# Linear attention: key decays of all eight sub-blocks by one subtraction and one exponential per direction, no clears by GpSimd

## The chip, the cores and the metric

One Trainium2 chip, one core of it. The metric is the device time of the whole program in microseconds (us), the median of several executions. The core's engines work side by side and wait for one another through semaphores: TensorE (PE, matrix products; its weight loads are PEld), VectorE (DVE), ScalarE (ACT), GpSimd (POOL) and SyncE (SP, which only issues transfers here).

## The reference, cut to what matters

The program is two model blocks, one after the other, over 512 tokens of width 1024. The first has two layers (`l` = 0, 1). Each layer mixes tokens in four branches (a short convolution, gated linear attention, latent attention, a wide convolution), and then runs a feed-forward network. The second block has a state-space mixer and a mixture of 32 experts. The change concerns only the gated linear attention of the two layers, which runs in both directions over the sequence:

```python
b = jnp.cumsum(ac, axis=2)                      # running sum of log decays, per key channel
rel = b[:, :, :, None, :] - b[:, :, None, :, :]
decay = jnp.where(mask5, jnp.exp(jnp.where(mask5, rel, 0.0)), 0.0)
scores = jnp.einsum('bhtk,bhsk,bhtsk->bhts', qc, kc, decay)
```

Four heads of 32 key channels lie on the 128 partitions. A score of query t and key s is a sum over channels of q·k·exp(b[t] − b[s]). To make it a matrix product, the exponential is split at an anchor a: exp(b[t] − b[a]) goes to the query, exp(b[a] − b[s]) to the key.

## The kernel before, in words

Tokens lie along the free dimension in four blocks of 128 (`j` = 0 to 3, `TB` = 4), and inside a block in eight sub-blocks of 16 (`SUB`, `NSUB`), each with an anchor of its own. `cpos` holds the running sums of both directions `d`, and `kdec[:, d, i, s]` the key decays of direction d against the anchor of sub-block i, for the 128 keys of the block: 128 partitions x 1024 elements per direction.

The order of work is written out by hand: each engine has one instruction stream, in program order, and nothing overtakes. For each `j` the streams are:

- **ScalarE** (lines 1317 to 1360): for both directions eight exponentials into `kdec`, one for each sub-block (L1327), each with the anchor as its bias and only over the keys that the sub-block may see (16, 32, ... 128 columns). For j = 0 they wait for GpSimd's clear of that half of `kdec`, later for the products that read it (`gdiag` of j − 1). Then the exponentials `khat` and `qhat` for the pairs of different blocks (L1337, L1340), then at j = 0 and 1 copies of values (L1282), then the copies of the off-diagonal scores from PSUM (L1352, L1357), which wait for TensorE. At j = 2 the copy of a projection `gg0` (L1235) comes behind them; at j = 3 three square roots (L1202) come ahead of them.
- **VectorE** (lines 1960 to 2009): `kdec` is bounded and multiplied by the keys in one instruction per direction (L1965, `scalar_tensor_tensor` with `min` and `mult`), then `khat` and `qhat` are multiplied (L1973, L1976). Then comes side work: `centre` at j = 0, squares at j = 1 and 2 (L1990), modulation values at j = 2 (L1726). Then the diagonal scores are masked out of PSUM (L1998) and the two directions added (L2003). L2009 marks that all scores are there.
- **TensorE** (lines 741 to 782): values of the tokens (`token_values`), a mean, then for each j eight products `gdiag` per direction (a 128 x 128 slice of `kdec` against 64 columns of `qdiag`), the off-diagonal `goff`, and side work behind them: `token_values` at j = 0, `modulation` (weights against 2 columns) at j = 1, the projection `gg0` at j = 2, `gg1` at j = 3. At j = 3 three variances stand between `gdiag` and `goff`. All of these have line 589 in the profile, where the helper `mm` records them. A float32 product stands in the trace as two records.
- **GpSimd** (lines 456 to 462): clears `qdiag`, and then the two halves of `kdec`, once per layer (L460 and L462). The never-written parts of `kdec` stay zero from then on. The region of `kdec` is shared with the buffers `score` and `probs` of the softmax attention that runs before, so the second clear waits for the last transposition (`turn`, L734), which reads `probs`.

`BOUND` is 1e30. The mask of L1998 sets every score of a forbidden pair to zero.

Of the kernel before, what the change touches and what calls it, by code (L numbers as in the profile page):

```python
# [9 lines left out]
P = 128  # L10
T = 512
TB = T // P
# [5 lines left out]
HEADS = 4  # L18
# [5 lines left out]
SUB = 16  # L24
# [111 lines left out]
def build(nc, io, marks, found):  # L136
    with ExitStack() as ctx:
# [311 lines left out]
        def _(pool):  # L449
# [6 lines left out]
            for l in range(DEPTH):  # L456
                pool.wait_ge(dve_done, when("query", l, HEADS - 1))
                nc.gpsimd.memset(qdiag, 0.0).then_inc(pool_done, did.up(("qdiag_zero", l)))
                pool.wait_ge(act_done, when("exps", l, HEADS * TB - 1))
                nc.gpsimd.memset(kdec[:, 0], 0.0).then_inc(pool_done, did.up(("kdec_zero", l, 0)))  # L460
                pool.wait_ge(pe_done, when("full", "turn", l, HEADS * TB - 1))
                nc.gpsimd.memset(kdec[:, 1], 0.0).then_inc(pool_done, did.up(("kdec_zero", l, 1)))  # L462
            pool.wait_ge(pe_done, when("full", "up", DEPTH - 1, KF - 1, 1))
            pool.dma_start(hc, io["ctx"].rearrange("p (k t) -> p k t", t=CTX)).then_inc(s_ctx, 16)
            pool.wait_ge(act_done, when("norm_out", ("ln2", DEPTH - 1), KD - 1))
# [722 lines left out]
        def _(act):  # L1188
# [42 lines left out]
            for l in range(DEPTH):  # L1231
# [84 lines left out]

                for j in range(TB):
                    for d in range(2):
                        if j == 0:
                            act.wait_ge(pool_done, when("kdec_zero", l, d))  # L1320
                        else:
                            act.wait_ge(pe_done, when("full", "gdiag", l, j - 1, d))
                        for i in range(NSUB):
                            a = j * P + i * SUB + (0, SUB - 1)[d]
                            s0, s1 = ((0, (i + 1) * SUB), (i * SUB, P))[d]
                            act.wait_ge(act_done, did.n)
                            nc.scalar.activation(kdec[:, d, i, s0:s1], cpos[:, d, j * P + s0:j * P + s1], ACT.Exp,  # L1327
                                bias=cpos[:, d, a:a + 1], scale=-1.0).then_inc(act_done, did.up(*([("kdec_exp", l, j,
                                d)] if i == NSUB - 1 else [])))
                    for d in range(2):  # L1330
                        if 0 < (TB - 1 - j, j)[d]:
                            a = (j * P + P - 1, j * P)[d]
                            t0, t1 = (((j + 1) * P, T), (0, j * P))[d]
                            if j >= 2:
                                act.wait_ge(pe_done, when("full", "goff", l, j - 2, HEADS - 1))
                            act.wait_ge(act_done, did.n)
                            nc.scalar.activation(khat[:, d, j % 2, :], cpos[:, d, j * P:(j + 1) * P], ACT.Exp,  # L1337
                                bias=cpos[:, d, a:a + 1], scale=-1.0).then_inc(act_done, did.up())
                            act.wait_ge(act_done, did.n)
                            nc.scalar.activation(qhat[:, d, j % 2, t0:t1], cpos[:, d, t0:t1], ACT.Exp, bias=cneg[:,  # L1340
                                d, a:a + 1]).then_inc(act_done, did.up(("qhat_exp", l, j, d)))
                    if j < 2:
                        keep_values(2 * j)
                    if j == TB - 1:
                        for i, tag in enumerate((("cfm", l), ("branch", l, 0), ("branch", l, 2))):
                            deviation(tag, out=deviations[:, i, :])
                    for h in range(HEADS):
                        act.wait_ge(pe_done, when("full", "goff", l, j, h))
                        src = bank_of("goff", l, j, h)
                        if j > 0:  # L1350
                            act.wait_ge(act_done, did.n)
                            nc.scalar.activation(amat(h)[:, j, 0:j * P], src[:, 0:j * P],  # L1352
                                ACT.Copy).then_inc(act_done, did.up(*([("free", "goff", l, j,
                                h)] if j == TB - 1 else [])))
                        if j < TB - 1:
                            act.wait_ge(act_done, did.n)
                            nc.scalar.activation(amat(h)[:, j, (j + 1) * P:T], src[:, (j + 1) * P:T],  # L1357
                                ACT.Copy).then_inc(act_done, did.up(("free", "goff", l, j, h)))
                    if j == TB - 2:
                        keep("gg0")  # L1360
# [356 lines left out]
        def _(dve):  # L1717
# [109 lines left out]
            for l in range(DEPTH):  # L1827
# [127 lines left out]
                for c in range(2):  # L1955
                    dve.wait_ge(dve_done, did.n)
                    nc.vector.tensor_tensor(y[:, c, :], y[:, c, :], proj[:, SLOT["b0"] + c, :],
                        ALU.mult).then_inc(dve_done, did.up(("ya", l)))

                for j in range(TB):  # L1960
                    kj = proj[:, SLOT["k"], j * P:(j + 1) * P]
                    for d in range(2):
# [20 lines left out]
                    if j in (1, 2):  # L1983
                        dve.wait_ge(act_done, when("yc", l, HEADS - 1))
                        for tag, src, dst in (((("cfm", l), proj[:, 0:2, :], early_squares["cfm"]),
                                               (("branch", l, 0), y[:, 0:2, :], early_squares[0])) if j == 1 else
                                              ((("branch", l, 2), y[:, 4:6, :], early_squares[2]),)):
                            for k in range(2):
                                dve.wait_ge(dve_done, did.all_but(1))
                                nc.vector.tensor_tensor(dst[:, k, :], src[:, k, :], src[:, k, :], ALU.mult).then_inc(  # L1990
                                    dve_done, did.up(("square", tag, k)))
                        dve.wait_ge(dve_done, did.n)
                    for d, mask in enumerate((const("upto"), const("after"))):
                        dve.wait_ge(pe_done, when("full", "gdiag", l, j, d))
                        src = bank_of("gdiag", l, j, d)[:].rearrange("p (i h t) -> p h i t", h=HEADS, t=SUB)
# [728 lines left out]
```

## Time and profile before

| | us |
|---|---|
| median of 3 runs | 3659.97 (3656.41 to 3660.52) |
| the profiled execution, its own time | 3656.11 |
| its span in the trace | 3654.3 |
| PE busy | 3439.4 (94%) |
| DVE busy | 2409.4 (66%) |
| ACT busy | 1713.0 (47%) |
| POOL busy | 492.3 (13%) |

All times of rows are counted from the start of the span. The linear attention of layer 0 lies at about 245 to 330 us, that of layer 1 at about 1065 to 1150 us. In a timeline a row is: start, duration, engine, line, operation, output and inputs, shapes, count; in brackets how long the engine was idle before it, and what ended that. Granted clock 1.00 is 2.4 GHz of TensorE, 0.50 is 1.2 GHz.

### The profile page before, as it was taken

The page shows a single profiled execution, that of the slowest core. Times are in us where ns is not written, and L with a number is a line of the kernel's source. Part 1 is how long each engine was busy: PE and PEld are TensorE (multiplying, and loading weights), DVE is VectorE, ACT ScalarE, POOL GpSimd, SP SyncE. Part 2 cuts the span into 40 slices and gives each one's busy share as a digit, 9 for nine tenths or more (in the row PEclk, how much of TensorE's full clock was granted, in tenths as well). Part 3 has the DMA queues.
Part 4 walks back from the last instruction along what each step waited for, and adds up shares of the span by engine and source line. Part 5 has one row for each costly group of instructions (what it writes and reads, how often), then busy time and mean ns, then how long its engine had stood idle before and what let it go on. Part 6 is the DMA issues. An engine that isn't in the chain of part 4 may idle for free.

```text
span 3654.3 us, 43770 instructions
## 1 busy us (share of the span) xinstructions
PE 3439.4 (94%) x13658; PEld 2393.2 (65%) x13658; DVE 2409.4 (66%) x2948; ACT 1713.0 (47%) x2318; POOL 492.3 (13%) x630
## 2 busy tenths in 40 slices
PE   7989999999988999998998889989999999999996
PEld 3445588874344588875654554378887888888884
DVE  3565464553564464555556874179999999999995
ACT  2344232232344332233321113168888888888884
POOL 0000000000000000000000000024343433334340
PEclk9988999999988999999998999999999999999998
DMA  4100233332110233332111002169999999999995
GB/s 180 52 31 28 81 116 115 113 101 69 52 35 23 87 112 113 116 114 71 52 52 58 24 24 92 63 245 372 355 375 347 369 367 365 369 355 376 352 372 182
DMA packets 167697, 618.86 MB, mean 169 GB/s; under 512 B 18496, under 2 KB 18624, under 8 KB 166880
## 3 DMA queue, kind: packets, MB, share of 16 engines
q1 hardware_dynamic: 156768, 573.84, 43.7%
q0 software_dynamic: 10816, 43.52, 4.2%
q8 instruction: 70, 1.15, 0.1%
q14 instruction: 43, 0.35, 0.0%
HBM read 587.92 MB, written 29.36 MB: 169 GB/s over the span
## 4 chain that ended last, share of the span: by engine, by line
PE 53%; issue 21%; POOL 11%; DVE 9%; ACT 3%; POOLq 2%; DMA 1%; DVEq 0%; SPq 0%; ACTq 0%
PE bank L589 51%; POOL pick L555 2%; POOL sb_work L501 2%; POOL y_rows L561 1%; DVE sb_rstd L1737 1%; DVE sb_work L1779 1%; POOL sb_work L507 1%; POOL picks_e L508 1%; POOL sb_work L547 1%; POOLq L514 1%; POOL sb_work L549 1%; POOLq L513 1%; ACT sb_work L1327 1%; POOL sb_work L544 1%; DVE sb_work L2259 0%
## 5 line engine op out<-in xcount | busy, mean ns | idle before, releaser
L2462 DVE TENSOR_TENSOR w_part<-sb_ring,w_part 128x1024 fp32r<-128x1024 f32 x762 | 890.1, 1225 | 63.1 <-ACT w_part L1641 38.9
L1641 ACT ACTIVATE w_part<-sb_ring 128x1024 fp32r<-128x1024 f32 x762 | 770.5, 1054 | 80.5 <-PE bank L1126 47.7
L1126 PE MATMUL bank<-w_part,xg_hi 128*128 128x512 f32 x2048 | 564.1, 397 | 0.0
L589 PE MATMUL bank<-h_hi,split_part 128*128 128x512 f32 x1408 | 447.5, 403 | 4.8 <-ACT h_hi L1409 4.8
L1126 PEld LDWEIGHTS bank<-w_part,xg_hi 128*128 128x128 f32 x2048 | 383.1, 188 | 89.1
L589 PE MATMUL bank<-sb_work,sb_ring 128*128 128x512 f32 (+5 forms) x880 | 331.4, 531 | 4.0 <-ACT sb_rstd L1202 2.5
L1126 PE MATMUL bank<-w_part,xg_lo 128*128 128x512 f32 x1024 | 321.2, 395 | 0.0
L589 PEld LDWEIGHTS bank<-h_hi,split_part 128*128 128x128 f32 x1408 | 267.2, 191 | 69.2 <-ACT h_hi L1409 5.1
L1126 PE MATMUL bank<-w_part,act_hi 128*128 128x512 f32 x1024 | 284.9, 400 | 2.0 <-DVE act_lo L2505 0.9
L589 PE MATMUL bank<-sb_hT,sb_ring 128*128 128x512 f32 (+1 forms) x608 | 272.5, 606 | 9.6 <-ACT sb_hT L1218 9.6
L589 PE MATMUL bank<-h_lo,split_part 128*128 128x512 f32 x704 | 272.1, 393 | 0.0
L589 PEld LDWEIGHTS bank<-sb_work,sb_ring 128*128 128x128 f32 (+4 forms) x880 | 162.8, 187 | 163.1 <-issue 150.6
L589 PE MATMUL bank<-sb_work 128*128 128x64 f32 (+6 forms) x992 | 228.8, 414 | 30.9 <-DVE sb_work L1965 13.7
L589 PE MATMUL bank<-act_hi_ff,split_part 128*128 128x512 f32 x704 | 229.9, 408 | 5.7 <-DVE act_lo_ff L2089 5.7
L1402 ACT ACTIVATE split_part<-sb_ring 128x1024 fp32r<-128x1024 f32 x136 | 142.7, 1052 | 194.2 <-PE bank L589 194.2
L1126 PEld LDWEIGHTS bank<-w_part,xg_lo 128*128 128x128 f32 x1024 | 192.6, 188 | 46.5
L589 PEld LDWEIGHTS bank<-sb_hT,sb_ring 128*128 128x128 f32 (+1 forms) x608 | 116.6, 193 | 160.2 <-issue 157.9
L1126 PEld LDWEIGHTS bank<-w_part,act_hi 128*128 128x128 f32 x1024 | 187.4, 188 | 45.4 <-issue 4.3
L1449 ACT ACTIVATE sb_work<-bank 128x512 f32<-128x512 f32 x88 | 52.7, 599 | 339.4 <-PE bank L589 335.9
L589 PEld LDWEIGHTS bank<-sb_work 128*128 128x128 f32 (+3 forms) x992 | 141.6, 218 | 100.1 <-issue 44.8
L589 PE MATMUL bank<-sb_xT,sb_ring 128*128 128x512 f32 (+2 forms) x416 | 187.9, 607 | 11.8 <-ACT sb_xT L1218 11.8
L2047 DVE TENSOR_TENSOR split_part<-sb_ring,split_part 128x1024 fp32r<-128x1024 f32 x136 | 165.9, 1221 | 20.2 <-ACT split_part L1402 20.0
(350 smaller groups left out, 4630.2 us busy)
## 6 DMA issues: line engine op xcount, KB each, us to landing
sb_ring<-in_w SPq DMA_DIRECT2D x768, 512.0 KB, 7.4
sb_ring<-in_wstream SPq DMA_DIRECT2D x304, 512.0 KB, 3.5
y_rows<-sb_padc POOLq DMA_DIRECT2D x1, 4096.0 KB, 27.4
sb_xT<-in_x SPq DMA_DIRECT2D x1, 2048.0 KB, 11.6
x_rows<-sb_padc SPq DMA_DIRECT2D x1, 2048.0 KB, 22.7
residual<-sb_hT POOLq DMA_DIRECT2D x1, 2048.0 KB, 6.6
sb_hT<-residual POOLq DMA_DIRECT2D x1, 2048.0 KB, 8.2
x_rows<-sb_work SPq DMA_DIRECT2D x1, 2048.0 KB, 7.0
```

Of the source, the lines that this page charges most:

```text
L501: nc.gpsimd.tensor_tensor(passed[:, n:n + 1], slot_row[:, 0:1], slot_row[:, 0:1], ALU.add).then_inc(moe_pool_done, turn_did.up())
L507: nc.gpsimd.tensor_copy(rank_e.unsqueeze(2), rank[:, :, bass.ds(e, 1)]).then_inc(mark, turn_did.up())
L508: nc.gpsimd.tensor_copy(picks_e[:], picks[:, :, bass.ds(e, 1), :].bitcast(F32).rearrange("p b e c -> p b (e c)")).then_inc(mark, turn_did. ...
L513: e = pool.value_load(table[0:1, 0, bass.ds(i + ahead, 1)], min_val=0, max_val=EXPERTS - 1)
L555: nc.gpsimd.tensor_scalar(pick[:, b, :], slots, rank_e[:, b:b + 1], None, ALU.is_equal).then_inc(moe_pool_done, turn_did.up(("pick",)))
L589: ins = nc.tensor.matmul(out, l, r, start=start, stop=stop)
L1126: ins = nc.tensor.matmul(out[n][:], l[:, k, :], r[:, n * 512:(n + 1) * 512], start=False, stop=(k, p) == (KD - 1, 2))
L1402: nc.scalar.activation(split_hi[t % NSPLIT], ring[:, n % RING, :], ACT.Copy).then_inc(act_done, did.up(("w_hi", l, t)))
L1449: nc.scalar.activation(ubuf[:, i % 4, 1:T + 1], bank_of("up", l, c, v)[:], ACT.Copy).then_inc(act_done, did.up(("free", "up", l, c, v), (" ...
L1641: nc.scalar.activation(w_hi[t % SPLITS], ring[:, t % RING, :], ACT.Copy).then_inc(s_hi, 1)
L2047: nc.vector.tensor_tensor(split_lo[t % NSPLIT], ring[:, n % RING, :], split_hi[t % NSPLIT].bitcast(F32), ALU.subtract).then_inc(dve_done, ...
L2462: nc.vector.tensor_tensor(w_lo[t % SPLITS], ring[:, t % RING, :], w_hi[t % SPLITS].bitcast(F32), ALU.subtract).then_inc(s_lo, 1)
```

## The change

GpSimd no longer clears `kdec`. A new function `key_args(j)` on VectorE subtracts, in one instruction per direction, the anchors of all eight sub-blocks from the block's 128 running sums, into all 1024 elements of `kdec[:, d]`. ScalarE then takes one exponential per direction over these 1024 elements, in place, with no bias. `key_args(0)` stands ahead of the loop over j on VectorE; `key_args(j + 1)` stands in turn j behind the side work and ahead of the masks of L1998. It waits for the products that read `kdec` (`gdiag` of the turn before it), or for j = 0 for the last transposition. The positions that used to stay zero now get an exponential as well, which L1965 bounds and the mask removes.

```diff
@@ gpsimd
-                pool.wait_ge(act_done, when("exps", l, HEADS * TB - 1))
-                nc.gpsimd.memset(kdec[:, 0], 0.0).then_inc(pool_done, did.up(("kdec_zero", l, 0)))
-                pool.wait_ge(pe_done, when("full", "turn", l, HEADS * TB - 1))
-                nc.gpsimd.memset(kdec[:, 1], 0.0).then_inc(pool_done, did.up(("kdec_zero", l, 1)))
@@ scalar
                 for j in range(TB):
                     for d in range(2):
-                        if j == 0:
-                            act.wait_ge(pool_done, when("kdec_zero", l, d))
-                        else:
-                            act.wait_ge(pe_done, when("full", "gdiag", l, j - 1, d))
-                        for i in range(NSUB):
-                            a = j * P + i * SUB + (0, SUB - 1)[d]
-                            s0, s1 = ((0, (i + 1) * SUB), (i * SUB, P))[d]
-                            act.wait_ge(act_done, did.n)
-                            nc.scalar.activation(kdec[:, d, i, s0:s1], cpos[:, d, j * P + s0:j * P + s1], ACT.Exp,
-                                bias=cpos[:, d, a:a + 1], scale=-1.0).then_inc(act_done, did.up(*([("kdec_exp", l, j,
-                                d)] if i == NSUB - 1 else [])))
+                        act.wait_ge(dve_done, when("kdec_arg", l, j, d))
+                        nc.scalar.activation(kdec[:, d], kdec[:, d], ACT.Exp, scale=-1.0).then_inc(act_done,
+                            did.up(("kdec_exp", l, j, d)))
@@ vector
+                def key_args(j):
+
+                    for d in range(2):
+                        pos = cpos[:, d, j * P:(j + 1) * P]
+                        anchor = pos.rearrange("p (i s) -> p i s", s=SUB)[:, :, (0, SUB - 1)[d]:(1, SUB)[d]]
+                        if j == 0:
+                            dve.wait_ge(pe_done, when("full", "turn", l, HEADS * TB - 1))
+                        else:
+                            dve.wait_ge(pe_done, when("full", "gdiag", l, j - 1, d))
+                        dve.wait_ge(dve_done, did.n)
+                        nc.vector.tensor_tensor(kdec[:, d], pos.unsqueeze(1).to_broadcast([P, NSUB, P]),
+                            anchor.to_broadcast([P, NSUB, P]), ALU.subtract).then_inc(dve_done,
+                            did.up(("kdec_arg", l, j, d)))
+
+                key_args(0)
                 for j in range(TB):
...
+                    if j + 1 < TB:
+                        key_args(j + 1)
                     for d, mask in enumerate((const("upto"), const("after"))):
                         dve.wait_ge(pe_done, when("full", "gdiag", l, j, d))
```

## Rows read from the trace of the kernel before

**Rows 1.** Page of the profile: the chain that ended last, by engine.

```profile
PE 53%; issue 21%; POOL 11%; DVE 9%; ACT 3%; POOLq 2%; DMA 1%; DVEq 0%; SPq 0%; ACTq 0%
```

**Rows 2.** L1965 in both layers: its waits, then its waiters (us, times).

```profile
  ACT sb_work L1327: 74.3, 16
...
  PE bank L589: 13.7, 6
```

**Rows 3.** Timeline of PE, layer 0.

```profile
244.79 5.53 PE L589 MATMUL bank<-sb_work 128*64 128x512 f32 x8 [0.69 <-ACT sb_work L1267]
...
273.43 3.13 PE L589 MATMUL bank<-sb_work 128*128 128x64 f32 x32 [1.07 <-DVE sb_work L1965]
...
284.10 8.70 PE L589 MATMUL bank<-sb_work 128*128 128x64 f32 x48 [0.63 <-DVE sb_work L1965]
292.73 8.95 PE L589 MATMUL bank<-sb_hT,sb_ring 128*128 128x512 f32 x16
...
328.52 4.13 PE L589 MATMUL bank<-sb_sq,sb_work 128*64 128x512 f32 x13
```

**Rows 4.** Timeline of ACT, layer 0.

```profile
250.37 0.59 ACT L1274 ACTIVATE sb_xT<-bank 64x512 f32<-64x512 f32 x1 [5.62 <-PE bank L589]
251.05 6.24 ACT L1327 ACTIVATE sb_work<-sb_work 128x16 f32<-128x16 f32 x16
...
265.87 6.24 ACT L1327 ACTIVATE sb_work<-sb_work 128x16 f32<-128x16 f32 x16
...
279.66 6.24 ACT L1327 ACTIVATE sb_work<-sb_work 128x16 f32<-128x16 f32 x16
...
302.41 6.23 ACT L1327 ACTIVATE sb_work<-sb_work 128x16 f32<-128x16 f32 x16
```

**Rows 5.** Timeline of DVE, layer 0.

```profile
243.07 1.42 DVE L1957 TENSOR_TENSOR sb_xT<-sb_xT,sb_work 128x512 f32<-128x512 f32 x2
...
272.14 1.23 DVE L1965 SCALAR_TENSOR_TENSOR sb_work<-sb_work 128x1024 f32<-128x1024 f32 x1 [1.88 <-ACT sb_work L1327]
...
305.56 1.22 DVE L1965 SCALAR_TENSOR_TENSOR sb_work<-sb_work 128x1024 f32<-128x1024 f32 x1 [12.65 <-ACT sb_work L1327]
...
323.92 0.06 DVE L2009 MEMSET sb_work<- 128x1 f32 x1 [8.27 <-ACT sb_work L1352]
```

**Rows 6.** The chain that ended last, behind the last wait: start, us, what.

```profile
306.84 33.52 PE bank L589 x102
```

**Rows 7.** Costs: two lines of the page (mean ns), three of the lines' own views.

```profile
L2462 DVE TENSOR_TENSOR w_part<-sb_ring,w_part 128x1024 fp32r<-128x1024 f32 x762 | 890.1, 1225 | 63.1 <-ACT w_part L1641 38.9
L1641 ACT ACTIVATE w_part<-sb_ring 128x1024 fp32r<-128x1024 f32 x762 | 770.5, 1054 | 80.5 <-PE bank L1126 47.7
...
L1327 ACT ACTIVATE sb_work<-sb_work x128: 307/356/405, 251.1 to 1128.0; 128x16 f32<-128x16 f32 x16, 128x32 f32<-128x32 f32 x16, 128x48 f32<-128x48 f32 x16, 128x64 f32<-128x64 f32 x16
...
L1313 ACT ACTIVATE sb_sq<-sb_sq x4: 619/620/621, 201.9 to 1023.5; 128x512 f32<-128x512 f32 x4
...
L462 POOL MEMSET sb_work<- x2: 952/952/952, 244.2 to 1064.3; 128x1024 f32 x2
```

**Rows 8.** Windows: us, busy PE, PEld, DVE, ACT, POOL, then granted clock, DMA share, GB/s.

```profile
258.99:262.70 3.71, 3.71 (x37) 3.64 (x35) 2.53 (x4) 0.34 (x1) 0.00 (x0) 1.00 0.00 0
...
276.49:283.47 6.98, 6.98 (x35) 6.89 (x32) 3.75 (x7) 6.10 (x18) 0.00 (x0) 0.50 0.23 73
...
292.73:296.40 3.67, 3.67 (x9) 1.60 (x6) 0.17 (x1) 2.65 (x8) 0.00 (x0) 0.50 0.01 2
296.45:301.69 5.24, 5.23 (x13) 2.01 (x11) 0.00 (x0) 0.00 (x0) 0.00 (x0) 1.00 0.00 0
301.69:306.84 5.15, 0.00 (x1) 0.00 (x1) 1.22 (x1) 4.61 (x13) 0.00 (x0) 0.98 0.00 0
306.84:313.72 6.88, 6.88 (x32) 6.88 (x33) 2.77 (x4) 3.96 (x8) 0.00 (x0) 0.50 0.24 76
313.72:321.46 7.74, 7.74 (x22) 3.10 (x22) 1.54 (x3) 2.06 (x3) 0.00 (x0) 0.79 0.00 0
```

## The prediction

> **What bounds the kernel now.** I read the page first. PE holds 53% of the chain that ended last [rows 1], so an edit on other engines pays only where PE waits for them. Next I read who waits for whom around the line whose input changes, L1965. In both layers together VectorE waits 74.3 us for the exponentials of L1327, but PE waits for L1965 only 13.7 us, in six places [rows 2]. That 13.7 us is the ceiling of what the shortened path can give by itself, since the 74.3 us are mostly VectorE having nothing else to do.
>
> The timeline of PE gives the places for layer 0: an idle of 1.07 us before 273.43, one of 0.63 us before 284.10 [rows 3], and the hole of 5.15 us from 301.69 to 306.84 [rows 8]. They sum to 6.85 us, half of 13.7, so layer 1 has the same three. Elsewhere between 244.79 and 301.69 PE is fed. Behind 306.84 the chain stays on PE for 33.52 us [rows 6]. PE's next user of the stage's results waits for the mark of L2009, which is set at 323.92 [rows 5], 4.6 us before PE comes to it in its own order, at 328.52 [rows 3]. So a PE that gets there earlier keeps what it gained, because the mark moves with PE's own products.
>
> The third view is the granted clock. It is 1.00 in the products of j = 0 and 0.50 in the modulation, and it falls at the end of the hole, to 0.50 for the products of j = 3 [rows 8]. The same 32 records of `gdiag` take 3.71 us at 1.00 and 6.88 us at 0.50 [rows 8]. The clock is therefore worth as much as the waits.
>
> **GpSimd's clears: 0 us.** The later one of layer 0 starts at 244.2 and lasts 0.95 us [rows 7], so it is over at 245.2. The first exponential starts at 251.05, directly behind the copy L1274 that waited for PE [rows 4]. What hides the clears is PE's product from 244.79; without that cover the later one would cost 0.95 us per layer.
>
> **The subtraction.** It is 128 x 1024 with two inputs. The nearest row is L2462, the same size and operation, 1.225 us [rows 7]; L1965 itself, one of whose inputs is a broadcast, has 1.23 us [rows 5]. I take 1.23 us. A far upper bound is four times that, 4.9 us, if inputs read over and over ran worse than any row here. Below, nothing speaks for less than 1.0 us. Two per turn make 2.5 us on VectorE, 19.7 us in all, and their place decides what they cost:
>
> - j = 0: VectorE is free at 244.5 [rows 5], the arguments are ready at 247, and the exponentials can start only at 251.05. Cost 0.
> - Turn 0, for j = 1: it waits for `gdiag`, which PE finishes at 260.9 and 262.7 (two halves of the stretch from 258.99 [rows 8]), so the arguments are ready at 262.1 and 263.9. ScalarE comes to them at 265.87, held by the copies of `goff` [rows 4]. Cost 0, with 1.9 us to spare on the second.
> - Turn 1, for j = 2: behind the squares, ready at about 276; ScalarE comes at 278.6 (279.66 less 1.07). Cost 0.
> - Turn 2, for j = 3: `gdiag` ends at about 290, ready at about 291; ScalarE comes at 302.4 less the gains. Cost 0.
>
> The masks of L1998 now queue behind this wait and these 2.5 us. Who waits for them is the bank of `gdiag`, needed again eight banks later, in the next turn, which is more than 5 us away. In turn 3 no `key_args` stands ahead of them. Cost 0.
>
> **The exponential.** For 1024 columns I bound it by 1.05 us, the activation of this size [rows 7], and 1.24 us, twice the 0.620 us of the exponential over 512 columns with no bias [rows 7]. The far bound is eight instructions of 128 columns, 8 x 0.405 = 3.2 us [rows 7]. I take 1.05 us, because 512 columns more cost 0.43 us by these rows and the fixed part is paid once. Both directions then take 2.2 us with their gaps, where 16 instructions take 6.24 us [rows 4].
>
> **The three waits, against the clock pattern of before.**
>
> 1. j = 1: exponentials from 265.87 end at 268.1, the second L1965 at 269.4. PE wants it at 273.43 − 1.07 = 272.36. The wait is gone: 1.07 us.
> 2. j = 2: PE leaves the modulation at 283.47 − 1.07 = 282.4. The input: ScalarE 278.6, + 1.05 + 0.06 + 1.23 + 0.05 = 281.0. That is hidden, and another 0.63 us gone.
> 3. j = 3: PE ends `gg0`, ScalarE copies it (301.69 to 302.41, 0.72 us [rows 4, 8]), then 1.05 + 0.06 + 1.23 + 0.05. The hole becomes 3.1 us where it was 5.15: 2.05 us. What is late next there is the copy of `gg0`, which stands ahead of the exponentials in ScalarE's order.
>
> Sum 3.75 us per layer, 7.5 us for both.
>
> **The clock.** Before, it is at 0.50 from 276.49 at the latest to 296.4, and from the end of the hole to about 317: the 7.74 us behind 313.72 have a mean of 0.79, which is 3.2 us at 0.50 and the rest at 1.00 [rows 8]. In the first stretch the gap of 1.07 us before the fall is gone, so more of the modulation can run at 1.00: each record of it then takes about half of its 0.22 us. Up to 1.4 us come of that, until the input of j = 2 (281.0, not 282.4) is the bound; I take 0.7 us. In the second, `gdiag` of j = 3 starts 3.1 us after PE's last work and not 5.15 us; of the 3.2 us between both clocks I take a third, 1.0 us. The two dense stretches (`gg0`, the variances) start at other points against the rise of the clock, worth ±1.5 us each, taken as 0.05 us together. That is 1.75 us per layer, 3.5 us for both. **Total 11 us.**
>
> The profiled execution's own time is 3656.1 us, so its counterpart is 3645 us. The median of the runs shown is 3.9 us above it, so for a median I say 3649 us. What a measurement of this kernel can tell from no change is about 0.2%, 7.3 us.
>
> **Rivals.**
>
> - **The clock gives nothing or takes a part back** (20%). The two stretches at 0.50 are as long as before relative to the work, or `gg0` and the variances begin just behind a chance to rise. Then 7.5 us less up to 4: 3652.5 to 3656 us, on the edge of no change. For it: the modulation, with its 2 columns, runs wholly at 0.50 already [rows 8]. Against: the hole is the one long idle, and it shrinks.
> - **The clock survives the hole** (12%). With 3.1 us of idle, `gdiag` of j = 3 stays at 1.00 (3.2 us), the variances too (their 3.2 us at 0.50 become 1.6 us), and the modulation gains 0.7 us. Per layer 3.75 + 5.5 = 9.3 us, 18.5 us in all: 3641 us. For it: PE stood idle from 301.69, and the mean of 0.98 over the hole says that the clock fell only at its very end [rows 8]. Against: `gdiag` fills the array thinly, and around 276 the clock fell after an idle of only 1.07 us [rows 3]. The Trainium skill, page "TensorE: Matmul & The Clock Gate", section "HAM oscillation — how this bites in real kernels", says that waits between short bursts make the clock fall back each time and that shorter gaps keep it up; by that rule this case would be the likeliest, and what the trace shows around 276 speaks against it.
> - **Slower: the clock stays at 0.50 through `gg0` and the variances** (4%). Place: the rise at 296.4 doesn't come. Price: the 5.24 us of `gg0` behind 296.45 double, +5.2; the 4.5 us at 1.00 of the variances and `goff` (317 to 321.5) double, +4.5. Less 3.75 that is +6 us per layer, 3672 us. It decides from +3.75 us per layer on, that is if one of the two rises is missed by most of its stretch. Against: `gg0` began at 292.73 and had the clock at 1.00 less than 4 us later [rows 8].
> - **The exponential is no cheaper in one piece** (4%): at 3.2 us each, the hole is 5.3 us, j = 2 starts later than before, j = 1 keeps its gain of 1 us. 3658 to 3660 us. A subtraction of 4.9 us alone would still be hidden in turn 2, and in turn 0 would eat the 1.07 us only. Against: the slope of rows 7.
> - That the change doesn't do what it says is excluded but for values: the added exponentials may overflow, L1965 bounds them and the mask removes them; no time hangs on values before the experts, and there only on the count of blocks.
>
> **How the numbers follow.** The forecast, 7.3 to 15 us off, has 60%; the rivals 20, 12, 4 and 4. Faster by over 0.2%: 60 + 12 = 72%. Within: 20 + 4 and a little of slower's near side, 24%. Slower: 4%. The range: 3641 (clock survives) up to 3657 us, which takes in the first rival and a drift of a median by a microsecond; left out are the last two, the far side of the clock's gain, and surprises.
>
> **What would show it.** In the profile after: exponentials 128 x 1024, 16 of them, at 1.05 us; subtractions 128 x 1024 at 1.23 us; no wait of PE for L1965 at j = 1, under 0.1 us at j = 2 or one that begins earlier, and a hole of 3.1 us at j = 3; no wait of ScalarE for the subtractions; the start of `gg0` 1.7 to 3 us earlier against the layer's start. Wrong would be: a wait of ScalarE for the subtraction, masks that hold a bank, a hole that stays near 5 us, or stretches at 0.50 longer than 20.5 and 10.2 us.

## The result, and the profile after

The changed kernel takes 3634.4 us (median of 4 runs), the kernel before 3658.2 us in the same runs. The ratio is 0.9946 [0.9933, 0.9959], and 0.9947 [0.9936, 0.9959] in a second, separate comparison. That is 0.53 to 0.54% faster, about 19.5 us (the two medians are 23.9 us apart, inside the first interval). Forecast were 11 us and a time of 3649 us with a range down to 3641 us: the sign was right, the size was not, and the range did not hold it. The chain that ended last is made up as before [rows 1]; the page of the changed kernel:

```profile
span 3637.2 us, 43670 instructions
...
PE 3425.6 (94%) x13658; PEld 2382.2 (65%) x13658; DVE 2428.7 (67%) x2964; ACT 1680.8 (46%) x2206; POOL 491.0 (14%) x626
...
PE 53%; issue 21%; POOL 11%; DVE 9%; ACT 3%; POOLq 2%; DMA 1%; DVEq 0%; SPq 0%; ACTq 0%
```

PE has the same 13658 records of matrix products in both kernels, so the two traces can be laid side by side by the count of the product. The timeline of PE, layer 0, after the change (it answers to [rows 3]):

```profile
246.00 5.55 PE L585 MATMUL bank<-sb_work 128*64 128x512 f32 x8 [0.69 <-ACT sb_work L1263]
...
271.68 4.57 PE L585 MATMUL bank<-sb_work 128*128 128x64 f32 x48
276.18 3.73 PE L585 MATMUL bank<-sb_csil,sb_ring 128*128 128x2 f32 x32
281.61 8.71 PE L585 MATMUL bank<-sb_work 128*128 128x64 f32 x48 [1.69 <-DVE sb_work L1968]
290.24 9.10 PE L585 MATMUL bank<-sb_hT,sb_ring 128*128 128x512 f32 x16
302.29 5.13 PE L585 MATMUL bank<-sb_work 128*128 128x64 f32 x32 [2.95 <-DVE sb_work L1968]
307.22 7.40 PE L585 MATMUL bank<-sb_work,sb_consts 128*128 128x512 f32 x12
```

The wait of 1.07 us is gone. The modulation (128x2) takes 3.73 us where it took 6.99 us. Behind it stands a wait that has *grown*, from 0.63 to 1.69 us, and the hole is 2.95 us where it was 5.15 us. Both waits end with VectorE's multiplication (L1965 before, L1968 after). The windows of the changed kernel show the clock of these pieces (columns as in [rows 8]):

```profile
276.18:279.88 3.70, 3.70 (x36) 3.65 (x32) 3.31 (x5) 3.23 (x9) 0.00 (x0) 1.00 0.10 27
281.61:288.60 6.99, 6.99 (x32) 6.90 (x32) 5.12 (x9) 1.38 (x4) 0.00 (x0) 0.50 0.26 77
302.29:307.22 4.93, 4.93 (x33) 4.93 (x33) 2.77 (x4) 1.97 (x3) 0.00 (x0) 0.72 0.37 106
307.22:315.41 8.19, 8.19 (x22) 3.26 (x22) 1.54 (x3) 2.06 (x3) 0.00 (x0) 0.75 0.00 0
```

The modulation ran wholly at 1.00, and `gdiag` of j = 3 in part; `gdiag` of j = 2, behind the modulation, is at 0.50 as before. The new operations have the lengths that were forecast, in their own views:

```profile
L1316 ACT ACTIVATE sb_work<-sb_work x16: 1043/1048/1057, 252.2 to 1110.0; 128x1024 f32<-128x1024 f32 x16
```

```profile
L1958 DVE TENSOR_TENSOR sb_work<-sb_work x16: 1224/1225/1226, 245.8 to 1098.2; 128x1024 f32<-128x1024 f32 x16
```

**Where the time went.** Windows from the values product of layer 0 to `gg1` of layer 0, from there to the values product of layer 1, the same stage in layer 1, and a stretch of the second block that has nothing to do with the change. The kernel before:

```profile
244.79:321.46 76.67, 69.81 (x313) 51.31 (x313) 28.11 (x45) 41.55 (x106) 0.33 (x1) 0.77 0.13 42
321.46:1064.97 743.51, 706.07 (x2642) 464.17 (x2638) 394.43 (x534) 222.97 (x330) 5.09 (x3) 0.97 0.26 82
1064.97:1140.90 75.93, 69.07 (x312) 51.28 (x312) 28.09 (x45) 41.56 (x106) 0.33 (x1) 0.78 0.13 42
2099.97:2199.95 99.98, 88.73 (x375) 58.09 (x375) 79.21 (x100) 21.73 (x41) 0.00 (x0) 0.95 0.06 22
```

The changed kernel, between the same products:

```profile
246.00:315.41 69.41, 64.77 (x313) 46.35 (x313) 37.70 (x53) 26.45 (x50) 0.00 (x0) 0.82 0.14 46
315.41:1055.95 740.54, 702.98 (x2643) 462.53 (x2639) 394.54 (x535) 222.80 (x330) 3.51 (x1) 0.97 0.27 83
1055.95:1124.60 68.65, 64.01 (x312) 46.23 (x312) 37.70 (x53) 26.45 (x50) 0.00 (x0) 0.83 0.14 46
2084.49:2180.64 96.15, 84.63 (x376) 55.17 (x376) 79.51 (x100) 21.70 (x41) 0.00 (x0) 1.00 0.06 23
```

The two stages give 7.26 and 7.28 us, 14.5 us. The part between them gives 2.97 us and the distant stretch 3.83 us, although PE, VectorE and ScalarE have the same work there. (Only GpSimd's two clears for layer 1 are gone from the part between, 5.09 to 3.51 us in its column; the experiment that puts them back shows that they don't count.) Between the second stage and the stretch 0.8 us are lost again. Left out are what lies ahead of the first stage, which differs by 1.3 us between two executions of the changed kernel, and what lies behind the stretch, with the expert loop: it takes 1454.4 and 1458.0 us in two executions of the kernel before, 1456.6 and 1451.1 us in two of the changed one, so nothing is read from it. The sum is 20.5 us and fits the 19.5 us of the ratio.

### The profile page after: what moved, and what is told of

Same layout as the page of the kernel before. It is cut to its first block, busy times and chain, and to the rows that moved or that the text cites. A ratio compares the mean times of both kernels' runs of the same rounds, so it can differ in the third digit from the quotient of the medians.

```text
span 3637.2 us, 43670 instructions
## 1 busy us (share of the span) xinstructions
PE 3425.6 (94%) x13658; PEld 2382.2 (65%) x13658; DVE 2428.7 (67%) x2964; ACT 1680.8 (46%) x2206; POOL 491.0 (14%) x626
## 4 chain that ended last, share of the span: by engine, by line
PE 53%; issue 21%; POOL 11%; DVE 9%; ACT 3%; POOLq 2%; DMA 1%; DVEq 0%; SPq 0%; ACTq 0%
PE bank L585 52%; POOL pick L551 3%; POOL sb_work L497 2%; POOL y_rows L557 1%; DVE sb_rstd L1725 1%; DVE sb_work L1767 1%; POOL sb_work L503 1%; POOL picks_e L504 1%; POOL sb_work L543 1%; POOLq L510 1%; POOL sb_work L545 1%; POOLq L509 1%; POOL sb_work L540 1%; DVE sb_turn_tables L2260 1%; DVE sb_work L2264 0%
## 5 line engine op out<-in xcount | busy, mean ns | idle before, releaser
L2052 DVE TENSOR_TENSOR split_part<-sb_ring,split_part 128x1024 fp32r<-128x1024 f32 x136 | 165.9, 1221 | 19.7 <-ACT split_part L1390 19.5
```

The source lines that it names most:

```text
L2052: nc.vector.tensor_tensor(split_lo[t % NSPLIT], ring[:, n % RING, :], split_hi[t % NSPLIT].bitcast(F32), ALU.subtract).then_inc(dve_done, ...
```

## The experiments

Theory A: the gain is made in the stage, by PE's waits and by what they do to the clock. Its rival: only the length of waits counts. Both leave the 6.8 us outside the stage open; theory P took that up later. "The stage" below is always from the values product to `gg1`, in layer 0 and layer 1.

### The changed kernel again

> The changed kernel unaltered, for a second trace and a better median. Theory A (all that counts happens inside the linear attention stage, through its waits and the clock there): the stage is again about 69.4 us in layer 0 and 68.7 us in layer 1 from the start of the values product to the start of gg1, and the time is below the kernel before by 15 to 20 us, because the 3 us that the first trace gained in the feed-forward part of layer 0 were one execution's clock. Theory B (the program as a whole gains more than the stage): again 22 to 26 us below the kernel before.

Ratio 0.9947 [0.9936, 0.9959]. The same windows of this second execution:

```profile
244.69:314.09 69.40, 64.76 (x312) 46.31 (x312) 37.68 (x53) 26.44 (x50) 0.00 (x0) 0.82 0.14 46
314.09:1054.62 740.53, 702.98 (x2642) 461.96 (x2638) 394.35 (x535) 222.79 (x330) 3.51 (x1) 0.97 0.27 83
1054.62:1123.29 68.67, 64.03 (x312) 46.21 (x313) 37.68 (x53) 26.45 (x50) 0.00 (x0) 0.83 0.15 46
2083.13:2179.24 96.11, 84.62 (x375) 55.13 (x375) 79.46 (x100) 21.70 (x41) 0.00 (x0) 1.00 0.07 23
```

Every stretch comes back to within 0.04 us. My expectation that the 3 us between the layers were one execution's clock was wrong: they come again with the same program.

### The kernel before again

> The kernel before, unaltered. Every theory: ratio 1 within the interval; stage 76.7 and 75.9 us, 743.5 us between the two stages and 99.98 us in the stretch of the second block, if these follow the program alone; if they change from one execution to the next by a microsecond or more, what was ascribed to the shift may be chance.

Ratio 1.0008 [0.9998, 1.0018]; stages 76.64 and 75.92 us, 743.51 us between them, 99.92 us in the stretch. So the traces differ by program, not by chance, and differences of 0.1 us in these windows can be read.

### The split at j = 1, and the split at j = 3

```diff
                         act.wait_ge(dve_done, when("kdec_arg", l, j, d))
+                        if j in (1,):
+                            for i in range(NSUB):
+                                nc.scalar.activation(kdec[:, d, i, :], kdec[:, d, i, :], ACT.Exp,
+                                    scale=-1.0).then_inc(act_done, did.up(*([("kdec_exp", l, j,
+                                    d)] if i == NSUB - 1 else [])))
+                            continue
                         nc.scalar.activation(kdec[:, d], kdec[:, d], ACT.Exp, scale=-1.0).then_inc(act_done,
                             did.up(("kdec_exp", l, j, d)))
```

The second kernel has `(3,)` in place of `(1,)`.

> At j = 1 each exponential of 1024 columns is eight of 128 columns, so PE's wait of about 1 us ahead of the second gdiag of j = 1 returns; nothing else changes. Theory A with the clock: the wait makes the clock fall before the modulation, which then takes 7 us where it took 3.7 us; PE reaches the products of j = 2 3 to 3.7 us later per layer, so the time is 6 to 7.4 us above the changed kernel. Rival (only the length of waits counts): 1 to 2.2 us above it, and the modulation stays near 3.7 us.

> The same split at j = 3 only: the hole before gdiag of j = 3 grows from 2.95 us to about 5.2 us. Theory A with the clock: gdiag of j = 3 takes 6.9 us where it took 4.9 to 5.4 us, so 3 to 4.2 us per layer and 6 to 8.4 us above the changed kernel. Rival (only the length of waits counts): 4.5 us above it, with gdiag unchanged in length.

Both missed their aim. PE's wait at j = 1 did not return, and the hole at j = 3 grew by 0.64 us and not by 2.2 us. The timeline of ScalarE in the split at j = 1 says why:

```profile
267.30 3.29 ACT L1318 ACTIVATE sb_work<-sb_work 128x128 f32<-128x128 f32 x16
```

Sixteen exponentials of 128 columns take 3.29 us, 0.206 us from one to the next. The kernel before needed 6.24 us for sixteen that were *smaller* [rows 4]. One difference is the wait on ScalarE's own semaphore ahead of each, which I had left out here; the other is the bias, which these have no more. The stages were 69.66 and 68.90 us (split at j = 1) and 70.05 and 69.29 us (at j = 3), ratios 0.9956 [0.9943, 0.9968] and 0.9956 [0.9943, 0.9969]: neither theory is tested, but a new one comes up (theory W): the cost of before was mostly the wait between one exponential and the next.

### The kernel before without these waits

```diff
                             s0, s1 = ((0, (i + 1) * SUB), (i * SUB, P))[d]
-                            act.wait_ge(act_done, did.n)
                             nc.scalar.activation(kdec[:, d, i, s0:s1], cpos[:, d, j * P + s0:j * P + s1], ACT.Exp,
```

> The kernel before, with one line less: between the eight exponentials of a direction (disjoint outputs, inputs long ready) ScalarE no longer waits for its own exponential before. If the cost of before was the drain of one activation ahead of the next, as 16 unwaited ones of 128 columns in 3.29 us suggest, the 16 exponentials take 2.5 to 3.4 us where they took 6.24 us, the wait of 1.07 us at j = 1 goes, the hole shrinks to 3.2 to 3.6 us, and the time is 14 to 22 us below the kernel before: most of what the change gave, without VectorE's subtractions. Rival (the number of instructions is what costs): still about 5 to 6 us for 16, and at most 6 us below before.

The timeline of its ScalarE and of its PE:

```profile
264.73 4.02 ACT L1326 ACTIVATE sb_work<-sb_work 128x16 f32<-128x16 f32 x16
```

```profile
274.02 3.73 PE L589 MATMUL bank<-sb_csil,sb_ring 128*128 128x2 f32 x32
280.45 8.70 PE L589 MATMUL bank<-sb_work 128*128 128x64 f32 x48 [2.70 <-DVE sb_work L1964]
...
301.63 6.52 PE L589 MATMUL bank<-sb_work 128*128 128x64 f32 x32 [3.96 <-DVE sb_work L1964]
```

One line less takes 2.2 of the 4.2 us that the change took off the sixteen exponentials, brings the modulation to full clock, and shortens the stages to 72.50 and 71.78 us: 8.3 us of the 14.5. The ratio is 0.9978 [0.9967, 0.9988], 8 us; it has the 3.85 us of the distant stretch (96.13 us) but not the 3 us between the layers (744.23 us). The exponentials were 4.0 us, between the 2.5 to 3.4 us that I expected and the 5 to 6 us of the rival, and the gain is below my 14 to 22 us. So "mostly" was too much: the wait is 2.2 of the 6.2 us, and the number of instructions costs as well. The Trainium skill bears on this, page "ScalarE: Activation LUTs", section "What ACT_TABLE_LOAD costs": an activation with immediate scale and bias has a fixed part of 186 ns, a bias read from memory adds 93 ns, activations back to back overlap by 93 ns, and a column takes 0.833 ns. An estimate from these figures is 0.20 us each without bias at 128 columns, and 0.25 us each with one at 72 columns in the mean. The trace agrees: 0.206 us each and 0.252 us each. With the wait between it is 0.390 us each (6.24/16), 0.14 us more. That this is the overlap lost and about 0.05 us besides is an estimate from the same figures.

### The wait at j = 1, brought back

The changed kernel with the split at j = 1 as above, and one line more in it:

```diff
+                            act.wait_ge(act_done, did.n)
                             nc.scalar.activation(kdec[:, d, i, :], kdec[:, d, i, :], ACT.Exp,
```

> The changed kernel with j = 1 split into eight exponentials of 128 columns per direction and ScalarE's own wait between them, so that PE's wait ahead of the second gdiag of j = 1 does return (1 to 1.6 us). Theory A with the clock: the clock falls about when the modulation begins, which takes 6 to 7 us where it took 3.7 us; PE reaches gdiag of j = 2 at 2.5 to 4 us later per layer. Rival (only waits count): 1 to 1.6 us later per layer, hidden in part by the wait of 1.69 us that stands behind the modulation, so 0 to 1 us.

The timeline of PE:

```profile
271.95 2.88 PE L585 MATMUL bank<-sb_work 128*128 128x64 f32 x32 [0.34 <-DVE sb_work L1975]
274.76 3.73 PE L585 MATMUL bank<-sb_csil,sb_ring 128*128 128x2 f32 x32
282.56 8.71 PE L585 MATMUL bank<-sb_work 128*128 128x64 f32 x48 [4.06 <-DVE sb_work L1975]
```

The wait came back at a third of its old length, and the clock did not fall ahead of the modulation, which stays at 3.73 us. So what a wait of 1 us does there was not tested. Yet PE reaches `gdiag` of j = 2 2.9 us later than in the changed kernel (2.37 us more of waiting, and 0.52 us by which the modulation starts later), because the data for it is late. Theory A's 2.5 to 4 us came out by luck, since the modulation kept its length. ScalarE's sixteen exponentials took 5.51 us, 0.344 us each: against 0.206 us without the wait that is 0.14 us again. The stages were 72.54 and 71.82 us, ratio 0.9977 [0.9966, 0.9989]. So a late input costs by itself, without a change of the clock ahead of it, and behind the modulation the data sets the time.

### Products in the hole of the kernel before

```diff
+                        out = bank("gdiag", l, j, d)
+                        if (j, d) == (TB - 1, 0):
+                            for _ in range(5):
+                                mm(out[:], ident, hT[:, 0, :], True, True)
                         pe.wait_ge(dve_done, when("kdec", l, j, d))
-                        out = bank("gdiag", l, j, d)
```

> The kernel before with five products of 512 columns, whose result nobody reads, put into the hole ahead of gdiag of j = 3 (written to the bank that gdiag then overwrites). They are extra work that fills the idle time and adds none. Theory A with the clock: gdiag of j = 3 runs at 1.00, 3.5 to 4 us where it took 6.9 us, and the variances lose their 3.2 us at 0.50: 4 to 5 us per layer, 8 to 10 us below before, with every wait as before. Rival (only the length of waits counts): no change, or slower by what the filler overruns the hole.

Ratio 0.9999 [0.9988, 1.0011]. Timeline of PE, and the windows of the two halves of `gdiag`:

```profile
303.96 4.45 PE L589 MATMUL bank<-sb_hT,sb_consts 128*128 128x512 f32 x10
309.28 2.00 PE L589 MATMUL bank<-sb_work 128*128 128x64 f32 x16 [0.86 <-DVE sb_work L1968]
312.48 3.65 PE L589 MATMUL bank<-sb_work 128*128 128x64 f32 x16 [1.20 <-DVE sb_work L1968]
```

```profile
309.28:311.20 1.92, 1.92 (x16) 1.86 (x16) 0.10 (x1) 1.70 (x6) 0.00 (x0) 1.00 0.00 0
312.48:315.90 3.42, 3.42 (x16) 3.42 (x17) 1.50 (x3) 1.09 (x1) 0.00 (x0) 0.50 0.00 0
```

The filler held the clock: the first half ran at 1.00. But the second half then waited 1.20 us for its own input, since the second eight exponentials come 3.2 us behind the first, and by then the clock had fallen. Together 6.63 us where it was 6.88 us. The rival's number came out (no change), for a reason that neither theory had: a full clock was worth nothing here, where the next input was late. The change shortens both, because each direction's exponential now takes 1.0 us.

### The subtractions made twice

```diff
+                        nc.vector.tensor_tensor(kdec[:, d], pos.unsqueeze(1).to_broadcast([P, NSUB, P]),
+                            anchor.to_broadcast([P, NSUB, P]), ALU.subtract).then_inc(dve_done, did.up())
+                        dve.wait_ge(dve_done, did.n)
                         nc.vector.tensor_tensor(kdec[:, d], pos.unsqueeze(1).to_broadcast([P, NSUB, P]),
```

> The changed kernel with each subtraction made twice, 2.5 us more per turn on VectorE. By the prediction's step (the subtractions are hidden in every turn, even at several times their cost) the stage stays within 1 us of 69.4. Theory V (behind the modulation PE waits for VectorE's own order: squares, two subtractions, masks, then the multiplication; 0.3 us of slack): no cost at j = 1, but gdiag of j = 2 starts 3 to 4.5 us later per layer, 6 to 9 us in all.

Stages 73.16 and 73.44 us. The timeline of VectorE in the unaltered changed kernel shows the queue that does it (squares, subtractions, masks, multiplication), and then PE's wait with the subtractions doubled:

```profile
274.89 2.55 DVE L1958 TENSOR_TENSOR sb_work<-sb_work 128x1024 f32<-128x1024 f32 x2
277.55 1.49 DVE L2003 TENSOR_TENSOR sb_work<-bank,sb_consts 128x512 f32<-128x512 f32 x2
...
280.33 2.55 DVE L1968 SCALAR_TENSOR_TENSOR sb_work<-sb_work 128x1024 f32<-128x1024 f32 x2 [0.30 <-ACT sb_work L1316]
```

```profile
284.98 8.70 PE L585 MATMUL bank<-sb_work 128*128 128x64 f32 x48 [5.74 <-DVE sb_work L1971]
```

The multiplication waited only 0.30 us for ScalarE: VectorE's own order is nearly the bound in that turn. Doubled, `gdiag` of j = 2 of layer 0 starts 4.07 us later, at j = 1 nothing is lost (4.50 us from `gdiag` of j = 1 to the modulation, as before the edit). Theory V holds. The time is 3650.7 us, ratio 0.9991 [0.9981, 1.0001]: more than the 8.5 us of the stages came back, because 745.67 us lie between them and 100.27 us in the stretch.

### GpSimd's clears put back

```diff
+                pool.wait_ge(act_done, when("exps", l, HEADS * TB - 1))
+                nc.gpsimd.memset(kdec[:, 0], 0.0).then_inc(pool_done, did.up(("kdec_zero", l, 0)))
+                pool.wait_ge(pe_done, when("full", "turn", l, HEADS * TB - 1))
+                nc.gpsimd.memset(kdec[:, 1], 0.0).then_inc(pool_done, did.up(("kdec_zero", l, 1)))
...
-                            dve.wait_ge(pe_done, when("full", "turn", l, HEADS * TB - 1))
+                            dve.wait_ge(pool_done, when("kdec_zero", l, d))
```

> The changed kernel with GpSimd's two clears of kdec back, at their old places, and the first two subtractions waiting for them in place of the transposition. Theory A, as predicted: no change, stage again 69.4 and 68.7 us, since the subtractions then end about 1 us later and have 3 us to spare. Rival (GpSimd's writes slow VectorE, or the wait matters): more than 1 us per layer.

Stages 69.38 and 68.64 us, 740.55 us between them, ratio 0.9950 [0.9934, 0.9967]. The clears cost nothing, as predicted, and their absence is not what shortened the part between the layers.

### Everything behind layer 1's stage moved back

```diff
+                    if (l, j) == (1, TB - 1):
...
+                        for n in [T] * 19 + [T // 2]:
+                            nc.tensor.matmul(out[:, 0:n], ident, hT[:, 0, 0:n], start=True, stop=True)
```

> The changed kernel with 16.65 us of dense products, whose result nobody reads, ahead of gg1 in layer 1 only, so that all that comes behind lies again where it lay in the kernel before. It is there for one stretch: the about 100 us in the second block that took 99.98 us before and 96.1 us in every other kernel so far. Theory P (the clock's changes are tied to the distance from the program's start, and this stretch lost a span at 0.50 by the shift alone): the stretch takes about 100 us again, and the clock shows a span of about 10 us at 0.50 in it. Rival (the change made that stretch faster in some other way): 96.1 us, and the time is 16.65 us above the changed kernel.

Ratio 0.9996 [0.9984, 1.0008]. The stretch took 96.13 us, not 100: theory P's forecast failed, and the rival's came out. But the aim was missed as well: the part on the way, from `gg1` of layer 1 to the stretch, became 3.2 us shorter (956.67 us where the changed kernel had 959.89), and the stretch was reached 3.0 us earlier than in the kernel before. By itself the run decides nothing. All kernels together say more. The distance is from the start of layer 0's values product to the start of the stretch:

| kernel | between the layers, us | distance, us | stretch, us |
|---|---|---|---|
| both waits taken away (last section) | 743.26 | 1821.5 | 96.16 |
| copy of gg0 later (next section) | 743.66 | 1828.2 | 96.11 |
| changed, three kernels: as it is, split at j = 1, clears back | 740.30 to 740.55 | 1838.4 to 1838.5 | 96.11 to 96.15 |
| changed, split at j = 3 | 743.33 | 1841.9 | 96.12 |
| before without ScalarE's own waits | 744.23 | 1848.6 | 96.13 |
| changed, wait at j = 1 brought back | 744.19 | 1848.7 | 96.15 |
| before with products in the hole | 740.20 | 1851.8 | 99.92 |
| changed, subtractions twice | 745.67 | 1851.8 | 100.27 |
| changed, moved back | 740.54 | 1852.1 | 96.13 |
| before (twice) | 743.51 | 1855.2 | 99.98, 99.92 |

Both lengths of the stretch occur with the new code and with the old, so the new code is not what made it faster. The same holds between the layers: the shortest time there is one of the old code with products in the hole, and the longest one of the new code. Two distances 0.3 us apart give different lengths. And the windows show that the clock goes with the difference; the first is of the kernel before without its own waits, the second of the changed kernel with the subtractions twice:

```profile
2092.45:2188.58 96.13, 84.62 (x375) 55.13 (x375) 79.19 (x100) 21.70 (x41) 0.00 (x0) 1.00 0.06 22
```

```profile
2097.11:2197.38 100.27, 88.70 (x375) 58.06 (x375) 79.48 (x100) 21.72 (x41) 0.00 (x0) 0.95 0.06 22
```

A mean of 0.95 over 100 us is 10 us at 0.50; at 1.00 the span is missing. So much of theory P stands: the same instructions have two lengths, by a span at 0.50 that is there or not. That timing chooses between them is argued, because no edit is common to the kernels of one length. Which timing gives which is not settled by these runs; the distance alone does not.

### The copy of gg0 behind the exponentials of j = 3

```diff
                     if j == TB - 1:
+                        keep("gg0")
                         for i, tag in enumerate((("cfm", l), ("branch", l, 0), ("branch", l, 2))):
...
-                    if j == TB - 2:
-                        keep("gg0")
```

> The changed kernel with ScalarE's copy of gg0 moved behind the exponentials of j = 3. The input of gdiag of j = 3 is then ready before PE ends gg0, so the hole of 2.95 us is gone. Theory A with the clock: gdiag of j = 3 runs at 1.00 (3.7 us for 4.9 to 5.4 us) and the variances lose their stretch at 0.50, so 4.5 to 6.5 us per layer, 9 to 13 us below the changed kernel. Rival (only waits): 5.9 us below it. If the hole was harmless because something behind it is late anyway: no change.

3625.3 us, ratio 0.9918 [0.9903, 0.9932]. The timeline of its PE:

```profile
291.03 9.11 PE L585 MATMUL bank<-sb_hT,sb_ring 128*128 128x512 f32 x16
299.98 3.68 PE L585 MATMUL bank<-sb_work 128*128 128x64 f32 x32
303.49 5.37 PE L585 MATMUL bank<-sb_work,sb_consts 128*128 128x512 f32 x12
```

No hole, `gdiag` at 3.51 us for 4.93 us, and the variances at full clock. The stages are 62.87 and 62.13 us, 6.5 us less each, of which 3.1 us are the hole and 3.4 us the clock. This is the test that the waits at j = 1 and the filler could not give: with the data in time, the clock is worth as much as the wait (one edit gives both, and the starts of the products tell them apart). Of the 13.1 us of the stages 3.1 us are lost between the layers (743.66 us for 740.54), so the time is only 7 to 11 us below the changed kernel (by the medians of the same runs and by the ratios), where I expected 9 to 13.

### Both waits that were left, taken away

ScalarE's exponentials of turn j + 1 stand ahead of its copies of turn j, and VectorE's masks of j = 1 behind the multiplication of j = 2:

```diff
+                    if j + 1 < TB:
+                        key_exps(j + 1)
                     for h in range(HEADS):
                         act.wait_ge(pe_done, when("full", "goff", l, j, h))
...
+                    if j == 2:
+                        masks(1)
...
+                    if j != 1:
+                        masks(j)
```

> The changed kernel with ScalarE's exponentials of turn j + 1 ahead of its copies of goff of turn j (and so ahead of gg0's), and VectorE's masks of j = 1 behind the multiplication L1968 of j = 2. Both waits of PE for L1968 that are left (1.69 us at j = 2, 2.95 us at j = 3) should go, and gdiag of j = 3 runs at 1.00: as late_gg0 (6.5 us per layer below the changed kernel) and up to 1.7 us more per layer at j = 2, so 13 to 16 us below the changed kernel by the stage. Rival: the copies of goff, now 2 us later, hold banks or khat, and take part of it back.

3616.9 us, ratio 0.9899 [0.9883, 0.9915]: 37 us below the kernel before, nearly twice the gain of the change. The stages are 18.8 us shorter than in the changed kernel, more than the 13 to 16 us that I expected. They are the first and the last line of these windows; the one between is PE's work behind the modulation of layer 0:

```profile
246.10:305.97 59.87, 59.87 (x313) 43.37 (x313) 37.70 (x53) 27.16 (x50) 0.00 (x0) 0.88 0.16 53
279.88:287.77 7.89, 7.89 (x50) 7.44 (x49) 6.83 (x14) 3.82 (x10) 0.00 (x0) 0.55 0.35 129
1049.23:1108.58 59.35, 59.35 (x312) 43.58 (x313) 37.70 (x53) 27.16 (x50) 0.00 (x0) 0.89 0.17 54
```

PE is busy for the whole of both stages. What is left in them is PE's own work and the clock: a mean of 0.88 over 59.87 us is 14 us at 0.50. The middle line shows part of them. The clock fell 0.8 us behind the end of the modulation, with no idle time at all before it. So in this stage an idle time is not needed for the clock to fall, and taking the waits away did not keep it up there.

## Why the prediction was wrong, step by step

- **The clears: 0.** Right; put back, they cost nothing.
- **The exponential: 1.05 us.** Right, 1.048 us. Why sixteen smaller ones took 6.24 us was not asked: a third or more of that was ScalarE waiting for itself, and one line less would have given 8.3 of the 14.5 us in the stages.
- **The subtraction: 1.23 us, hidden in every turn.** The price was right, and hidden it was. But the slack was overstated: in turn 1 I compared with ScalarE's arrival and did not follow the masks and the multiplication queued behind on VectorE, which leave 0.30 us. The rival with a subtraction of 4.9 us names turns 2 and 0 and leaves out turn 1, the one where it costs: with 2.5 us for each, the stages got 3.8 and 4.8 us longer, while turns 0 and 2 lost nothing.
- **The three waits.** j = 1: 1.07 us, right. j = 3: the hole is 2.95 us for 3.1, right. j = 2: I wrote that the wait goes. It grew to 1.69 us, because the modulation got faster than its successor's input ("one that begins earlier" stood only among the signs). PE reaches `gdiag` of j = 2 3.70 us earlier (35.61 us behind the values product for 39.31), where 1.70 + 0.7 us were forecast, and 3.1 us at the most: ScalarE came to the exponentials 1.7 us earlier and not 1.07.
- **The clock: 1.75 us per layer.** This is the term of the sum that was mis-sized. I took "0.7 us" for the modulation, and the whole of it ran at 1.00: 3.26 us off its length, 2.0 us of them net of the longer wait. I took "a third, 1.0 us" for `gdiag` of j = 3 and it gave 1.95 us; the variances took 0.45 us back. That is 2.0 + 1.95 − 0.45 = 3.5 us per layer where 1.75 us stood, and 7.3 us per stage for 5.5. As evidence against the clock's surviving I had used that it fell near 276 after an idle of only 1.07 us. It fell ahead of the modulation in all three kernels with an idle of 1.0 to 1.1 us there (before, before again, products in the hole), and behind it in all the others, with 0.34 us or none. It fell near the modulation in every kernel, in the last one (both waits taken away) without any idle. So the idle went with when it fell; that the idle causes the earlier fall fits all runs, but none gave the changed kernel the idle of 1 us back.
- **What lies behind the stage.** "A PE that gets there earlier keeps what it gained" was taken as a rigid shift of everything behind. It is not rigid: 3.0 us between the layers and 3.8 us in the second block came on top. This step was not in the sum or in the range at all. It is a third of the gain and the larger part of the miss: 6.8 us, where the clock in the stages was 3.5 us too small in all. Why these parts have the lengths that they have stays open, but for the spans at 0.50 seen in them.
- **The rivals.** "The clock survives the hole" had the nearest total (3641 us) but not the right cause: at j = 3 the clock did fall, at about 304.5, inside `gdiag` (mean 0.72). It was the modulation that it survived. The rule cited there from the Trainium skill, page "TensorE: Matmul & The Clock Gate", section "HAM oscillation — how this bites in real kernels", that shorter gaps keep the clock up, was borne out at j = 3 by the version without a hole (`gdiag` 3.51 us). At j = 2 it was not: with no gap at all the clock still fell behind the modulation (0.55 over the 7.89 us).

## What to carry to other kernels

Before pricing a run of short activations, ask whether each of them needs its wait for the one before it on its *own* engine. Here such a wait cost 0.14 us, more than the 72 columns of the mean activation (0.06 us by 307 to 405 ns over 112 columns [rows 7]), and leaving one line out gave 8.3 of the 14.5 us in the stages and 8 of the 19.5 us in all. Where PE waits a microsecond ahead of work of two columns, price the clock over the whole of that work, and then look whether the next input comes early enough to use it. And a forecast for a long program should not take the part behind an edit as rigid: a shift of 15 us went with changes of 3 to 4 us each in stretches hundreds of microseconds away.

## What was unexpected of the hardware

- The stretches of PE are the same to 0.1 us in two executions of one kernel, with the clock's changes in the same places, while a program shifted by a few microseconds can get other ones. The stretch of the second block has two lengths, 96.1 and 99.9 to 100.3 us, with a mean clock of 1.00 and 0.95. Not even the direction of a shift tells which: 1851.8 us of distance gave the long one and 1852.1 us the short one.
- A gap of 1.07 us, 3 us before work of two columns began, went with a fall of the clock and 6.99 us for that work; one of 0.34 us left it at 1.00 and 3.73 us. And with no gap at all the clock fell to 0.50 right behind this work.
- A wait for the end of ScalarE's own last activation, ahead of one that does not need its result, costs 0.14 us each time (0.390 for 0.252 us from start to start, and 0.344 for 0.206 us).
